# Odd attention's norms and scores between its gate units, an attention begun inside its projection, `ada` weight blocks spread over three projections, and a norm in two halves

## The reference

```python
# first block, odd layer: q, k, v, gate, qi, ki, wi = hn @ w_in
q = rms_norm(q.reshape(bsz, L, C_HEADS, C_HEAD_DIM), q_g)   # 8 heads of 128
k = rms_norm(k.reshape(bsz, L, C_KV_HEADS, C_HEAD_DIM), k_g)
att = dsa_attention(q, k, v, qi, ki, wi, rel_bias)          # each query keeps its top 64 keys
return (att * jax.nn.silu(gate)) @ w_out

# second block: every layer i, for the tokens (c) and for the context (c_ctx)
mod = jax.nn.silu(c) @ ada_w[i] + ada_b[i]                  # 6 x 1024 columns, shifts, scales, gates
h = modulate(x, norm_mix_g[i], sh1, sc1)
q, k, v = jnp.split(h @ w_qkv, [Q_DIM, Q_DIM + N_KV_HEADS * HEAD_DIM], axis=-1)
q, k = axial_rope(q, cos, sin), axial_rope(k, cos, sin)
p = softmax_with_sink(jnp.concatenate([s_ctx, s_win], axis=-1), sink)

# SSM mixer's end: y is 2048 wide, in 8 groups of 256
y = y.reshape(b, L, SSM_GROUPS_2, D_INNER // SSM_GROUPS_2) * jax.nn.silu(z).reshape(...)
y = rmsnorm(y, norm_g.reshape(SSM_GROUPS_2, -1))
return y.reshape(b, L, D_INNER) @ w_out
```

## Time and profile before

| | us |
|---|---|
| three runs | 1594.48, 1596.21, 1596.59 |
| median | 1596.21 |
| profiled execution, its own time | 1600.67 |
| profiled execution, span of its instructions | 1598.8 |
| TensorE busy | 1501.7 (94%) |
| VectorE, ScalarE, GpSimd busy | 731.6, 597.2, 278.5 |
| DMA | 206.84 MB |

### The profile page before, as it was taken

One profiled execution on the slowest core, in us unless ns is written; L12 is line 12 of the kernel. 1 busy time (PEld: TensorE's weight loads), 2 busy tenths in 40 slices (PEclk: granted clock), 3 DMA queues, 4 the chain that ended last, 5 costly groups with the idle time before them and its releaser, 6 DMA issues.

```text
span 1598.8 us, 22726 instructions
## 1 busy us (share of the span) xinstructions
PE 1501.7 (94%) x9424; PEld 1268.5 (79%) x9424; DVE 731.6 (46%) x1203; ACT 597.2 (37%) x1127; POOL 278.5 (17%) x224
## 2 busy tenths in 40 slices
PE   7899989989989998999999998999998999999997
PEld 6878789757845586888888886788997788899997
DVE  6762155424249834323223234764544762254453
ACT  4334144144327725122122224442443550243342
POOL 2000187002000010211011111344500120021111
PEclk9799999979989999999999999999999998999998
DMA  7412454676200023323222232132350332745450
GB/s 237 150 54 90 168 225 159 259 296 273 94 13 1 27 88 149 111 76 118 105 106 71 95 117 111 53 106 105 134 186 25 135 131 90 279 165 195 176 172 33
DMA packets 36109, 206.84 MB, mean 129 GB/s; under 512 B 4952, under 2 KB 9480, under 8 KB 14888
## 3 DMA queue, kind: packets, MB, share of 16 engines
q1 hardware_dynamic: 33344, 200.11, 34.6%
q10 hardware_dynamic: 1848, 2.52, 0.9%
q0 software_dynamic: 816, 2.78, 0.5%
HBM read 202.76 MB, written 2.62 MB: 128 GB/s over the span
## 4 chain that ended last, share of the span: by engine, by line
PE 84%; DVE 7%; ACT 3%; DMA 3%; issue 1%; POOL 1%; SPq 1%; ACTq 0%; POOLq 0%; DVEq 0%
PE lin L1740 17%; PE lin L1742 17%; PE lin L1741 17%; PE lin L1707 8%; PE lin L1852 3%; PE modp L1778 2%; DMA ring<-ada_in 2%; PE lin L2306 1%; PE lin L1723 1%; PE lin L2123 1%; PE lin L1724 1%; PE lin L1725 1%; PE aux L1794 1%; PE aux L1810 1%; PE aux L2223 1%
## 5 line engine op out<-in xcount | busy, mean ns | idle before, releaser
L606 DVE TENSOR_TENSOR w_split<-ring,w_split 128x1024 fp32r<-128x1024 f32 (+1 forms) x140 | 187.5, 1344 | 358.4 <-ACT w_split L601 358.0
L601 ACT ACTIVATE w_split<-ring 128x1024 fp32r<-128x1024 f32 (+1 forms) x140 | 157.9, 1133 | 412.2 <-PE lin L1742 362.7
L1740 PE MATMUL lin<-hn_hi,w_split 128*128 128x512 f32 (+1 forms) x768 | 265.0, 345 | 3.5 <-DVE w_split L606 3.5
L1742 PE MATMUL lin<-hn_hi,w_split 128*128 128x512 f32 (+1 forms) x768 | 264.6, 344 | 0.0
L1741 PE MATMUL lin<-hn_lo,w_split 128*128 128x512 f32 (+1 forms) x728 | 249.1, 342 | 0.0
L1740 PEld LDWEIGHTS lin<-hn_hi,w_split 128*128 128x128 f32 x768 | 145.8, 190 | 20.7 <-issue 3.6
L1742 PEld LDWEIGHTS lin<-hn_hi,w_split 128*128 128x128 f32 x768 | 146.0, 190 | 17.5
L1741 PEld LDWEIGHTS lin<-hn_lo,w_split 128*128 128x128 f32 x728 | 138.5, 190 | 15.7
L1741 PE MATMUL lin<-hid_split,w_split 128*128 128x512 f32 (+1 forms) x392 | 133.8, 341 | 0.0
L555 POOL TENSOR_TENSOR hn<-hn 128x256 f32<-128x256 f32 (+1 forms) x42 | 43.8, 1043 | 506.9 <-ACT hn L670 506.5
L1740 PE MATMUL lin<-hid_split,w_split 128*128 128x512 f32 (+1 forms) x352 | 118.5, 337 | 2.4 <-POOL hid_split L570 2.4
(11 more groups left out here) (422 smaller groups left out, 2953.7 us busy)
## 6 DMA issues: line engine op xcount, KB each, us to landing
ring<-ada_in SPq DMA_DIRECT2D x48, 1024.0 KB, 5.9
ring<-ssm_in_in SPq DMA_DIRECT2D x24, 1024.0 KB, 4.8
ring<-od_in_in SPq DMA_DIRECT2D x12, 1024.0 KB, 4.9
ring<-ffn0a_in_in SPq DMA_DIRECT2D x11, 1024.0 KB, 4.9
ring<-ffn0b_in_in SPq DMA_DIRECT2D x11, 1024.0 KB, 4.7
ring<-ffn1a_in_in SPq DMA_DIRECT2D x11, 1024.0 KB, 5.6
ring<-ffn1b_in_in SPq DMA_DIRECT2D x11, 1024.0 KB, 4.8
ring<-ev_in_in SPq DMA_DIRECT2D x9, 1024.0 KB, 13.1
```

The lines of the kernel that those rows point to most:

```text
L601: act.activation(parts[:, 0], w, ACT.Copy).then_inc(sig("w_high"), 1)
L606: dve.tensor_tensor(parts[:, 1], w, parts[:, 0].bitcast(F32), ALU.subtract).then_inc(sig("w_low"), 1)
L1740: mm(lin[0:m, tile % RING, 0:width], hi, x_hi, start=kt == 0, stop=False)
L1742: ins = mm(lin[0:m, tile % RING, 0:width], lo, x_hi, start=False, stop=kt == kts - 1)
```

## The change

- **Order of the loads.** The 28 `ada` blocks between `ev_out` and `w_o` stand differently: one behind each of the first four pairs of `od_in` blocks, eight behind `od_in` (20 before), two behind the second and two behind the third block of `od_out`, four behind it as before, and two and two inside `qkv`.
- **Odd layer.** Squares of k and q come after unit 15, their sums after unit 17, the spread rows and the turned v after unit 19, the scores after unit 21. The reciprocal stands inside the top-k rounds. The head norms are applied before the masks are written.
- **Second attention.** The rotations of k and of the first two pairs of q tiles, the turned v and the score products of pair 0 stand behind units 4, 6, 8, 9, 10 and 11 of `qkv`. The last two rotations go to `lin` banks after `qkv`, are copied by ScalarE into `rope_late`, and VectorE applies them in pairs 1 and 2.
- **Norm of y.** The sums are made for each half of the tiles, by products of 32 equal columns that land in four groups of 32 rows (`y_sums`). The square root and the reciprocal are taken over 128x256 (`y_root`, `y_inverse`), and the rows are spread by `y_rows`. `ssm_out` runs its first three tiles together over the first half, the second sums stand inside, and the other tiles follow.

```diff
 STREAM = [
-    ("ev_in", 9, 2 * KT * P), ("glu", 2, 4 * 4 * P), ("ev_out", 4, 2 * KT * P), ("ada", 4, 2 * KT * P),
-    ("od_small", 1, KT * SMALL), ("od_in", 12, 2 * KT * P), ("ada", 20, 2 * KT * P), ("od_out", 2, 2 * KT * P),
-    ("qkv", 2, 2 * KT * P), ("od_out", 2, 2 * KT * P), ("ada", 4, 2 * KT * P), ("qkv", 4, 2 * KT * P), ("w_o", 4, 2 * KT * P),
+    ("ev_in", 9, 2 * KT * P), ("glu", 2, 4 * 4 * P), ("ev_out", 4, 2 * KT * P), ("ada", 4, 2 * KT * P), ("od_small", 1, KT * SMALL),
+    ("od_in", 2, 2 * KT * P), ("ada", 1, 2 * KT * P), ("od_in", 2, 2 * KT * P), ("ada", 1, 2 * KT * P),
...
         def second_block_scalar(act, own):
-            act_norm(act, 2, 2 * L, "od_out", (0, 0, 0), True, later=6)
+            act_norm(act, 2, 2 * L, "od_out", (0, 0, 0), True,
+                     before=lambda kt: ada_copies(act, 4, 1) if kt == 6 else None, later=5)
...
+                if n == 6:
+                    ada_copies(act, 6, 1)
+                if n == 5:
+                    copies(act, "v_tok2", 2, lambda ps: ps,
+                           lambda n_: v_tok2[:, 2 * n_:2 * n_ + 2, :].rearrange("p a b -> p (a b)"))
+                if 9 <= n < 11:
+                    exps(0, n - 9)
+            for n in range(2):
+                tile = lin_of["rope_late"] + n
+                full(act, "lin", tile)
+                frees(act.activation(rope_late[:, n], lin[:, tile % RING, :].rearrange("p (a b) -> p a b", a=2), ACT.Copy),
+                      "lin", tile)
+            exps(0, 2)
...
+            def y_root(half_):
+                tile = aux_of[f"y_sums{half_}"]
+                full(act, "aux", tile)
+                frees(act.activation(y_roots[half_], aux[:, tile % AUX, 0:L], ACT.Sqrt, scale=1.0 / L, bias=eps[:]), "aux", tile)
+
             for n in range(DT_ - 6, DT_):
                 square_y(n)
-            roots(act, "y_norm", 2 * GROUPS, 1.0 / L)
+                if n == DT_ - 5:
+                    y_root(0)
+            y_root(1)
...
         def second_block_vector(dve, own):
+            for u in range(W_UNITS, 12):
+                weights_lo(dve, "qkv", u)
...
+                if u == 8:
+                    rope(0)
+                if u == 10:
+                    rope(1)
+            rope(2)
+            modulations(dve, own, 2, 5)
+            for j in range(3):
+                pair_maxima(0, j)
+            shares(0, 0)
+            for i in range(1, AT_PAIRS + 1):
                 if i < AT_PAIRS:
                     pair_maxima(i, 0)
-                if i > 0:
-                    shares(i - 1, 1)
+                shares(i - 1, 1)
+                if i < 3:
+                    rope(i + 2)
...
+            y_inverse(0)
             y_out(DT_ - 2)
             y_out(DT_ - 1)
+            y_normed(0)
+            y_inverse(1)
+            y_normed(1)
...
         # ScalarE, odd layer, inside the loop over the results of od_in
+                if n == 16:
+                    taken(act, "lin", lin_of["od_in"] + 15)
+                    own.mark(act.activation(sq1[:, 0:2, :], k1, ACT.Square))
+                    act.activation(sq1[:, 2:10, :], q1, ACT.Square).then_inc(sig("squares_qk1"), 1)
+                if n == 17:
+                    ada_copies(act, 1, 1)
+                if n == 18:
+                    roots(act, "kq_norm1", 20, 1.0 / P)
+                if n == 20:
+                    copies(act, "v_tok1", 1, lambda ps: ps, lambda n_: v_tok1.rearrange("p a b -> p (a b)"))
             softmax_exps(act, own, 1, (lh0, lh1), small, False)
...
         # VectorE, odd layer, in the rounds of the top-k
+                if r == TOPK // 16:
+                    inverses(dve, "kq_norm1", 20)
...
         # TensorE
                 between(n)
+                if n in (1, 3, 5, 7):
+                    ada(1)
+                if n == 8:
+                    ada_groups(1)
+                    pe.wait_ge(sig("squares_qk1"), 1)
+                    head_sums("kq_norm1", [[m] for m in range(10)], 1, lambda m: sq1[:, m, :])
+                if n == 9:
+                    head_rows("kq_norm1", 10, 1)
+                    tokens("v_tok1", lambda m: v1[:, m], 2)
+                if n == 10:
+                    for m in range(5):
+                        taken(pe, "aux", aux_of["over_kq_norm1"] + m)
+                    scores(1, lambda h, qt: q1[:, h, qt * P:(qt + 1) * P], lambda h: k1[:, h // 4, :])
             ada(4)
+            transposed_probs(1, (lh0, lh1))
             ada_groups(2)
...
-            linear("od_out", "od_out", 2, KT, lambda kt: q1[:, kt, :])
+            linear("od_out", "od_out", 2, KT, lambda kt: q1[:, kt, :], later=lambda n: ada(2) if 0 < n < 3 else None)
+            ada_groups(4)
...
+            def attention_begins(u):
+
+                if u == 3:
+                    ada_groups(5)
+                if u in (3, 5):
+                    ada(2)
+                if u == 7:
+                    ada_groups(6)
+                if u == 4:
+                    pe.wait_ge(sig("at_in"), 48)
+                    rotated(0)
...
+                if u in (6, 8):
+                    rotated(u // 2 - 2)
+                if u == 9:
...
+                    pair_scores(0, 0)
+                if u == 10:
+                    pe.wait_ge(sig("mod_read"), 2)
+                    pair_scores(0, 1)
+                if u == 11:
+                    pair_scores(0, 2)
...
+            def y_sums(half_):
+
+                tile = aux_of[f"y_sums{half_}"]
+                begin("aux", tile)
+                for part in range(2):
+                    for q in range(4):
+                        n = 8 * half_ + 2 * q + part
+                        pe.wait_ge(sig("y_squares"), n + 1)
+                        ins = mm(aux[32 * q:32 * q + 32, tile % AUX, 0:L], ones[:, 0:32], y_sq[:, n, :],
+                                 start=part == 0, stop=part == 1)
+                fills(ins, "aux")
...
+                if i == DT_:
+                    y_sums(0)
...
-            head_sums("y_norm", [[2 * n, 2 * n + 1] for n in range(GROUPS)], 1, lambda n: y_sq[:, n, :], "y_squares")
-            head_rows("y_norm", GROUPS, 1)
-            linear("ssm_out", "ssm_out", 1, DT_, lambda kt: ys[:, kt, :], ready=lambda kt: taken(
-                pe, "aux", aux_of["over_y_norm"] + kt // 4))
+            y_rows(0)
+            ssm_out_parts(range(3), range(4))
+            y_sums(1)
+            ssm_out_parts(range(3), range(4, 8))
+            y_rows(1)
+            ssm_out_parts(range(3), range(8, DT_))
+            for n in range(3, KT):
+                ssm_out_parts((n,), range(DT_))
```

More of the change, by code:

```diff
@@ L1709, in linear @@
                         fills(ins, "lin")
+                    if later is not None:
+                        later(n)
             def split_together(units, x, width, waits):
@@ L1751, in split_linear @@
                     split_unit(name, u, kts, x, width, waits=waits if u == 0 else None)
[L1752 to L1753 removed]
+                    if later is not None:
+                        later(u)
             ada_at = [0]
@@ L1781, in ada, with head_sums @@
                 ada_at[0] += blocks
-            def head_sums(name, groups, parts, src, squares=None):
+            def head_sums(name, groups, parts, src):
                 tile = aux_of[name]
```

220 lines of the change are left out of this document (123 added, 97 removed), and 2 rows, old and new, of the table AUX_TILES.

## The result

| | before | changed |
|---|---|---|
| median, us | 1596.4 (4 runs) | 1585.6 (4 runs, 1581.87 to 1587.76) |
| ratio | | 0.9933, interval 0.9921 to 0.9946 |
| profiled execution's span, us | 1598.8 | 1580.1 |
| TensorE busy, us | 1501.7 | 1485.1 |

The change is faster by 10.8 us. The forecast was 21.7 us; the time lies inside the stated range of 1566 to 1587, near its upper edge, but the gain is half of what was forecast.

What follows compares the result with a forecast made beforehand. TensorE, busy 94% of the span, was taken as the bound: only its idle, lower-clock and needless work could be won. Terms -14.0 + 10.0 - 5.8 - 11.9 = -21.7 took the median 1596.21 to 1574.5 us; range 1566 to 1587.

Steps and rivals of the forecast that it cites:

- part 3: In `qkv`: the second attention's start and four `ada` blocks placed inside the projection; -5.8 us, bounds -9 and -2.
- part 4: Before `ssm_out`: the y norm made in two halves; -11.9 us, bounds -13 and -8.
- the gate units end at 288.2 + 20.8: In `od_in`: 16.9 us of moved work and 3.9 of `ada` blocks delay the gate units' end to 309.0.
- So `od_out` starts at 337.3: After the odd layer's softmax: `od_out` starts at 337.3 instead of 351.3 us, -14.0.
- Part 1: Odd layer: norms, scores and softmax beside the gate units; -14.0 us, bounds -18 and -9.
- Cost +10.0: From `od_out`'s start to `qkv`'s first product: 47.1 us instead of 37.1, with waits of 3.9 and 1.6.
- the ring is too short: Rival: blocks wait for slots at all three projections, softmax and `od_out` terms at bad bounds; 1583.5 us, chance 0.15.
- VectorE is held by GpSimd: Rival: GpSimd's late weight splits hold VectorE's mask writing, delaying the odd scores by 10.6 us; 1584.8, chance 0.12.
- More is won: Rival: the clock stays high after the idle and the rotations hide; -30 us, 1566, chance 0.13.
- part 2: In `od_out`: `ada` blocks placed inside it; +10.0 us, +6 if loads come sooner, +14 if waits lower the clock.
- the clock stays low: Rival: `od_out`'s waits halve the clock through its last two blocks and three `qkv` units; +16, 1612 us, chance 0.04.
- half clock beyond the stretch near 320: Sign of being wrong: a granted clock at half outside the odd attention's stretch near 320 us.

Runs made afterwards that it cites:

- before_again: The kernel before, unedited, run again for another profile: 1595.34 us, ratio 0.9998.
- second profile: The changed kernel, unedited, run and profiled again: median 1584.06 us, ratio 0.992 to the kernel before.
- old_odd: Changed kernel with odd layer, `od_out` and `ada` order as before, early attention start and split y norm kept: 1574.49 us, ratio 0.9867.
- y_norm_only: Kernel before with only the y norm in halves added: 1584.82 us, ratio 0.9929.
- softmax_early: Changed kernel, odd-layer exponentials ahead of ScalarE's last two gate copies, four `ada` blocks between the output products: 1577.28 us, ratio 0.9884 to before.

## Why the prediction was off

The reasoning named the right work, waits and idle times in most places. It failed on what surrounds them: half clock, and what a move costs in stages that it priced at nothing. By the profiled spans, each against before_again:

| | forecast | first profile | second profile |
|---|---|---|---|
| `od_in` to `qkv` (parts 1 and 2) | -4.0 | +1.0 | -1.9 |
| `qkv` and attention (part 3, with the blocks) | -5.8 | -2.0 | -2.1 |
| y norm (part 4) | -11.9 | -12.0 | -12.0 |
| behind `ssm_out` | 0 | +2.6 | +2.0 |
| start, and all the rest | 0 | -0.6 | +1.6 |
| sum | -21.7 | -11.0 | -12.4 |

- **Part 4, -11.9.** Right: -12.2 as a change of its own. Inside its stages the profile gives 73.1 - 60.1 - 1.0 = 12.0; the reciprocal of 256 columns took 1.75 us, the estimate. The prediction did not ask whether the half clock of the old stage was chance. Before_again has it again, 0.61 over the sums and rows as in the first profile, so the whole of it was to be had.
- **Part 3, -5.8**, of which +3.8 were `ada` blocks, so -9.6 without them. As forecast, pair 1's first product follows `qkv` by 2.9 us (462.4 to 465.3); pair 3's comes 21.1 us behind it (20.4 forecast), and `qkv` took 78.5 where 67.7 + 10.9 = 78.6 was forecast. old_odd, which has part 3 without the blocks, gives for `qkv` and the attention together 203.0 against 212.7 in before_again: -9.7. Parts 3 and 4 were forecast at -21.5; old_odd measures -22.1.
- **Parts 1 and 2 with the blocks in `qkv`: -14.0 + 10.0 + 3.8 = -0.2.** This is the step that failed: by old_odd against the change they cost 9 to 11 us. My own terms said that the odd rebuild gains nothing, and I did not draw that sum. Within it:
  - "the gate units end at 288.2 + 20.8": the gate stage grew by 23.3 and 21.8 us in the two profiles, and was 101.3 to 104.6 in all kernels of this order, before's 79.5. The work was right; the half clock behind the head sums, 6.6 us in the one and 3.4 in the other, was not in it.
  - "So `od_out` starts at 337.3": from the gate units it took 27.5 and 26.9 us, 28.3 forecast. The idle (7.9) and its cause, the exponentials behind the last gate copies, were right. Part 1 as a whole came to -11.9 and -14.0 us, -14.0 forecast.
  - "Cost +10.0" for `od_out`: +12.9 and +12.1. The waits came to 5.1 us, 5.5 forecast; the half clock behind them, which stood only in the bound of +14, is the rest.
  - The four blocks in `qkv`: 3.8 of work, but old_odd's `qkv` and attention are 7.7 us shorter. Half clock in `qkv` (0.98) and the attention (0.97) stands against none. That the blocks bring it on is not shown.
- **How the loss divides.** Up to `w_o`'s end the two profiles of the change are 9.8 and 6.8 us longer than old_odd's. TensorE is idle there for 28.4 and 27.9 us, against 24.2: 4.2 and 3.8 us are waits. Read in slices of 1 us, it is busy at half clock for 30.0 and 25.2 us, against 18.2; at the gate units' 44% that is 5.2 and 3.1 us, by estimate. The two make up the difference. The medians say 1 to 3 us more, since both profiles of the change were among its shortest executions.
- **Stages costed at nothing.** From `ssm_out`'s end to the program's end it took 214.8 us before (both profiles) and 217.4 and 216.8 after. Most of it is half clock: 5.5 and 3.4 us of TensorE's busy time, where both profiles of before have none; for 3.4 us from about 1384 us on in both, and in the last norm, near 1569 us, in the first. The loads move little: `ssm_out`'s first three tiles now end together, the first slot is loaded again 22.9 us behind `ssm_out`'s start (6.9 before), and the last `ada` block is waited for (1.23 us against 0.31), but a wait of 0.68 behind it is gone. y_norm_only has 215.8, so part 4 alone does not bring all of it.
- **"The range ... the median of the runs is 1596.21, 4.5 below it, and so 1574.5."** The offset did no harm: it makes the forecast the median less 21.7. What the first profile had too much lies nearly all in the start and in two stretches at half clock, and no term counted those as won.

Of the rivals, "the ring is too short" (1583.5) comes nearest to the time, and rightly in its bound on `od_out`, but it put a loss of part 1 on slots, too. TensorE waited for no load inside `od_in`. "VectorE is held by GpSimd" did not occur: the mask adds ended at 292.9, and TensorE did not wait for the scores (its price has a slip: 1574.5 + 10.6 is 1585.1, not 1584.8). "More is won" takes +8 for part 2, whose good bound was +6. Of "the clock stays low" a part came, in stretches of 3 to 10 us and not through `od_out`'s last blocks and `qkv`; the prediction had named half clock beyond the stretch near 320 as a sign of being wrong.

Not settled: what brings the half clock on behind the head sums, at `qkv`'s beginning and in the attention.

## What to carry to other kernels

When work is moved out of an exposed stretch into a busy one, sum the terms of the move by itself before adding others: a gain of 35 us in one stage with 23, 13 and 4 given back elsewhere is no gain, and half clock on top makes it a loss. Look for what the mover leaves idle: here two orders of instructions (exponentials behind the last copies, weight splits behind the third result) were worth about 7 and, with the `ada` blocks in the idle time, 12 to 14 us against the change, more than the move itself. Take several profiles, or the clock of every timed run, before a stretch at half clock is booked as a gain.

## What the runs showed of the hardware

- The spread between executions of one kernel goes with the granted clock. Over six runs of the change the mean clock goes from 0.972 to 0.965 while the time goes from 1580.5 to 1590.7 us. It is not all clock: of the 7.7 us between the two profiles of before, 3.8 are idle time in the program's start.
- Half clock did not cost half of the time. Products of 128x256 in a gate unit followed each other at 0.21 us at 1.2 GHz and at 0.12 us at 2.4 GHz.
- Half clock came with stretches where TensorE idled (7.9 us before the transposes, 5.1 us of waits in `od_out`); with the idle at 0.6 us in softmax_early, the stretch ran at 1.00. It came also behind the 20 products of the head sums, which have no idle time, and 3.5 us into the 32 of the old y norm, from where it lasted until shortly before the end of the rows. Products of 24 columns in place of one left the stage at 101.3 us and the lower level where it was.
- Eight products of 32 result rows each, in four row groups, summed eight tiles of 128x256 squares in 1.0 us. The 32 products of one column had taken 10.6 us for sixteen such tiles, 7 of them at half clock.
